# Delta rule of a hybrid encoder block: the inverse kept on the other half of the partitions than its transpose, PSUM banks exchanged

## The chip, the core and the metric

The kernel runs on one core of a Trainium2 chip. The core has a matrix engine (TensorE, PE in the rows, its weight loads PEld), VectorE (DVE), ScalarE (ACT), GpSimd (POOL) and SyncE (SP), which here issues most transfers. TensorE reads both operands from SBUF, where a tile lies on up to 128 partitions, and writes PSUM, which has eight banks. The operand's partitions choose the rows of the array that a product uses, the output's partitions choose its columns. So a product of 64 rows and 64 columns uses one quarter of the array. The metric is device time in microseconds of one execution; lower is better.

## The reference

One encoder block over 1024 tokens of 1024 channels: layer norm and modulation, one input projection, two mixers (gated delta rule, window attention), gates, output projection, layer norm, a hierarchical mixture of experts, layer norm. What the change touches is the delta rule. In chunks of 64 tokens and for 8 heads it needs the solution of a unit lower triangular system:

```python
decay = jnp.where(causal, jnp.exp(jnp.where(causal, gdiff, 0.0)), 0.0)
lower = jnp.where(strict, jnp.einsum('bnhid,bnhjd->bnhij', k_beta, kc) * decay, 0.0)
tmat = lower + jnp.eye(CHUNK, dtype=f32)
u = lax.linalg.triangular_solve(tmat, v_beta, left_side=True, lower=True, unit_diagonal=True)
w = lax.linalg.triangular_solve(tmat, k_beta * jnp.exp(gc)[..., None],
                                left_side=True, lower=True, unit_diagonal=True)
attn = jnp.einsum('bnhid,bnhjd->bnhij', qc, kc) * decay
...
v_new = u_n - jnp.einsum('bhcd,bhde->bhce', w_n, state)
```

followed by a state of 128x128 per head that goes from chunk to chunk.

## The kernel before

`delta_rule` takes the tokens in eight steps `c` of 128 tokens. Each step holds two chunks of 64 tokens, one on partitions 0 to 63 and one on 64 to 127 (`rows[0]` and `rows[1]`, line 1124), for eight heads side by side. All of it is float32.

The inverse T of the triangular matrix is built by doubling. `t_` holds T, `tt` holds its transpose. Both start from the 2x2 blocks on the diagonal: `lower` on VectorE makes `ln` (the negated lower matrix, line 1423), masks it (line 1425) and adds the identity to give `t_` (line 1427). `turn` on TensorE (line 1211) transposes it, and ScalarE copies it to `tt` (line 1343). Then five levels follow. A level `k` is:

1. TensorE: `cm` (the part of `ln` that belongs to the level, line 1418) times `tt`, into bank `g` (line 1223), for head groups `g` = 0 and 1 of four heads each.
2. ScalarE: copy of that to `nsb` (line 1348), one copy for each `g`.
3. TensorE, for each `g`: the update of `tt` (line 1234, `t_` by `nsb`) into the left half of bank 2+g, and for levels 1 to 4 the update of `t_` (line 1238, `nsb` by `t_`) into the right half of the same bank.
4. VectorE, for each `g`: add the two to `tt` (line 1442) and `t_` (line 1444).

Every product here has 64x64 weights and 64 moving columns. A product of chunk 0 reads partitions 0 to 63 and writes 0 to 63, one of chunk 1 reads and writes 64 to 127, so all products of the levels use the two quarters on the diagonal of the array. A float32 product is issued as two weight loads and two matmuls, so 8 products (4 heads, 2 chunks) are 16 matmuls in the trace.

Between the levels the order on TensorE, written out by hand at lines 1288 to 1312, puts the recurrence of the step before: `read_state` (line 1269) before level 1 and after level 2, `write_state` (line 1281 for the state, line 1284 for the output) after levels 1 and 3, `turn_output` (line 1259) and `value_rows` (line 1246) after level 4, and `key_rows` (line 1253) after level 5. Then come `similarities` (line 1186), `solutions` (lines 1194 and 1201) and `turn` of the next step. Line 1284 takes its operands from one half of the partitions and writes the other half (`rows[1 - s]`): it uses one of the two quarters off the diagonal. ScalarE copies the output rows after levels 2 and 4 (`output_rows`, line 1362), which `turn_output` needs. In step 0 VectorE also finishes a convolution (line 1473), whose result goes to DRAM and comes back as the value tiles that `value_rows` reads. GpSimd scales the queries (line 1536) and the state (line 1528). Engines are in step through semaphores alone.

Of the kernel before, what the change touches and what calls it, by code (L numbers as in the profile page):

```python
# [11 lines left out]
ALU = mybir.AluOpType  # L12
# [14 lines left out]
LEVELS = 6  # L27
# [1067 lines left out]
def delta_rule(nc, m, a):  # L1095

    with ExitStack() as ctx:
# [6 lines left out]
        cm, at = m.sb("level_parts", [P, 2, H, CHUNK], ctx=ctx), m.sb("attention_t", [P, 2, H, CHUNK], ctx=ctx)  # L1104
        t_, tt, nsb, ttb, ttw = chunked("inverse"), chunked("inverse_t"), chunked("level_product"), chunked("inverse_t_beta"), chunked("inverse_t_gc")
# [9 lines left out]
        S = lambda name: sems[name]  # L1115
# [6 lines left out]
        v_in = [m.sem(f"delta_v_in{side}") for side in range(2)]  # L1122
        ps = m.ps
        rows = [slice(0, CHUNK), slice(CHUNK, P)]
        ps4 = lambda b: ps[:, b, :].rearrange("p (h t) -> p h t", h=4)
        ps8 = lambda b: ps[:, b, :].rearrange("p (h t) -> p h t", h=H)
        part4 = lambda b, half: ps[:, b, half * 256:half * 256 + 256].rearrange("p (h t) -> p h t", h=4)
        heads = lambda g: slice(4 * g, 4 * g + 4)
        at8 = lambda h: slice(h * CHUNK, (h + 1) * CHUNK)
        at4 = lambda h, half=0: slice(half * 256 + (h % 4) * CHUNK, half * 256 + (h % 4 + 1) * CHUNK)  # L1130
# [5 lines left out]
        over = lambda name, k=0: m.const(name)[:, k * CHUNK:(k + 1) * CHUNK].rearrange("p (o t) -> p o t", o=1).to_broadcast([P, H, CHUNK])  # L1136
# [39 lines left out]
        def _(pe):  # L1176
# [27 lines left out]
            def turn(c):  # L1204
                pe.wait_ge(S("t0_ok"), c + 1)
                if c >= 1:
                    pe.wait_ge(S("n_ok"), c * 10)
                for g in range(2):
                    for h in range(4 * g, 4 * g + 4):
                        for r in rows:  # L1210
                            last = pe.matmul(ps[r, g, at4(h)], t_[r, h, :], m.const("ident_chunk")[r, :], start=True, stop=True)
                    last.then_inc(S("tt_mm"), 1)

            def level(c, k):
                pe.wait_ge(S("cm_ok"), c * 5 + k)
                for g in range(2):
                    if k == 1:
                        pe.wait_ge(S("tt0_ok"), c * 2 + g + 1)
                    else:
                        pe.wait_ge(S("tt_ok"), c * 10 + 2 * (k - 2) + g + 1)  # L1220
                    for h in range(4 * g, 4 * g + 4):
                        for r in rows:
                            last = pe.matmul(ps[r, g, at4(h)], cm[r, k % 2, h, :], tt[r, h, :], start=True, stop=True)  # L1223
                    last.then_inc(S("n_mm"), 1)
                if k == 1:
                    pe.wait_ge(S("ln_ok"), c + 1)
                    pe.wait_ge(S("at_ok"), c + 1)
                for g in range(2):
                    pe.wait_ge(S("n_ok"), c * 10 + 2 * (k - 1) + g + 1)
                    if k > 1:  # L1230
                        pe.wait_ge(S("t_ok"), c * 8 + 2 * (k - 2) + g + 1)
                    for h in range(4 * g, 4 * g + 4):
                        for r in rows:
                            last = pe.matmul(ps[r, 2 + g, at4(h)], t_[r, h, :], nsb[r, h, :], start=True, stop=True)
                    if k < LEVELS - 1:
                        for h in range(4 * g, 4 * g + 4):
                            for r in rows:
                                last = pe.matmul(ps[r, 2 + g, at4(h, 1)], nsb[r, h, :], t_[r, h, :], start=True, stop=True)
                    last.then_inc(S("x_mm"), 1)

            def value_rows(c):
# [46 lines left out]
            for c in range(TC):  # L1288
                similarities(c)
                if c >= 1:  # L1290
                    solutions(c - 1)
                turn(c)
                if c >= 1:
                    read_state(c - 1, 0)
                level(c, 1)
                if c >= 1:
                    write_state(c - 1, 0)
                level(c, 2)
                if c >= 1:
                    read_state(c - 1, 1)  # L1300
                level(c, 3)
                if c >= 1:
                    write_state(c - 1, 1)
                level(c, 4)
                if c >= 1:
                    turn_output(c - 1)
                if c >= 1:
                    value_rows(c)
                level(c, 5)
                if c == 0:  # L1310
                    value_rows(c)
                key_rows(c)
# [88 lines left out]
        def _(dve):  # L1401
# [13 lines left out]
            def part(c, k):  # L1415
                if k >= 3:
                    dve.wait_ge(S("n_mm"), c * 10 + 2 * (k - 2))
                nc.vector.tensor_tensor(cm[:, k % 2], ln[:], over("level", k), ALU.mult).then_inc(S("cm_ok"), 1)

            def lower(c):  # L1420
                dve.wait_ge(S("scaled_ok"), c + 1)
                dve.wait_ge(S("kk_mm"), c + 1)
                nc.vector.tensor_tensor(ln[:], ps8(2), ds_[:], ALU.mult).then_inc(S("ln_ok"), 1)
                dve.wait_ge(S("ln_ok"), c + 1)
                step(nc.vector.tensor_tensor(cm[:, 0], ln[:], over("level", 0), ALU.mult))
                step.settle()
                nc.vector.tensor_tensor(t_[:], cm[:, 0], over("ident_chunk"), ALU.add).then_inc(S("t0_ok"), 1)
                part(c, 1)
                dve.wait_ge(S("qk_mm"), c + 1)
                dve.wait_ge(S("dt_ok"), c + 1)  # L1430
                if c >= 2:
                    dve.wait_ge(S("o_mm"), 2 * (c - 1))
                nc.vector.tensor_tensor(at[:, c % 2], ps8(3), dt_[:], ALU.mult).then_inc(S("at_ok"), 1)

            def level(c, k):
                if k < LEVELS - 1:
                    if k == 1:
                        dve.wait_ge(S("t0_ok"), c + 1)
                    part(c, k + 1)
                for g in range(2):  # L1440
                    dve.wait_ge(S("x_mm"), c * 10 + 2 * (k - 1) + g + 1)
                    nc.vector.tensor_tensor(tt[:, heads(g), :], part4(2 + g, 0), tt[:, heads(g), :], ALU.add).then_inc(S("tt_ok"), 1)
                    if k < LEVELS - 1:
                        nc.vector.tensor_tensor(t_[:, heads(g), :], part4(2 + g, 1), t_[:, heads(g), :], ALU.add).then_inc(S("t_ok"), 1)

            def decayed_keys(c):
                dve.wait_ge(S("tok_mm"), c * 2 + 2)
# [34 lines left out]
            scale_decays(0)  # L1482
            for c in range(TC):
                lower(c)
                if c == 0:
                    for t in range(3):
                        convolve_last(0, t)
                if c >= 1:
                    new_values(c - 1, 0)
                level(c, 1)  # L1490
                if c == LAST - 1:
                    split_gates_low(nc, m, dve, 0, slice(0, 1))
                if c >= 1:
                    new_state(c - 1, 0)
                if c == 0:
                    convolve_last(1, 0)
                level(c, 2)
                if c == 0:
                    convolve_last(1, 1)
                if c == LAST - 1:  # L1500
                    split_gates_low(nc, m, dve, 0, slice(1, 2))
                if c >= 1:
                    new_values(c - 1, 1)
                level(c, 3)
                if c == 0:
                    convolve_last(1, 2)
# [1026 lines left out]
def build(nc, a, out):  # L2533
    with ExitStack() as ctx:
# [20 lines left out]
        with ExitStack() as mid:  # L2555
# [6 lines left out]
            with ExitStack() as early:  # L2562
# [25 lines left out]
                m.gate_in = [nc.alloc_semaphore(name=f"w_gates_in{n}") for n in range(2)]  # L2588
                m.gate_hi, m.gate_lo, m.gate_mm = (nc.alloc_semaphore(name="gates_" + n) for n in ("high_ready", "low_ready", "summed"))
                delta_rule(nc, m, a)  # L2590
                attended.close()
                m.reuse_sems()
# [36 lines left out]
```

## Time and profile before

| what | value |
|---|---|
| runs | 2004.98 us median of 3 (2002.21 to 2007.64) |
| span of the profiled execution | 2006.3 us |
| TensorE busy | 1834.1 us, 91% |
| VectorE busy | 1433.6 us, 71% |
| ScalarE busy | 1071.1 us, 53% |
| GpSimd busy | 358.4 us, 18% |
| delta rule in the span | from 578.6 us to about 902 us |

For the profiled execution only the span is given, from its first to its last instruction; it lies 1.3 us above the median of the runs and inside their range, so differences of the span are taken as differences of the time. The granted clock of TensorE was 0.96 of full speed on average. The busy time of a matmul row runs to its modelled end, so of a dense run of matmuls the distance from start to start is to be read, not the mean duration. The rows read for the prediction stand below.

### The profile page before, as it was taken

The page shows a single profiled execution, that of the slowest core. Times are in us where ns is not written, and L with a number is a line of the kernel's source. Part 1 is how long each engine was busy: PE and PEld are TensorE (multiplying, and loading weights), DVE is VectorE, ACT ScalarE, POOL GpSimd, SP SyncE. Part 2 cuts the span into 40 slices and gives each one's busy share as a digit, 9 for nine tenths or more (in the row PEclk, how much of TensorE's full clock was granted, in tenths as well). Part 3 has the DMA queues.
Part 4 walks back from the last instruction along what each step waited for, and adds up shares of the span by engine and source line. Part 5 has one row for each costly group of instructions (what it writes and reads, how often), then busy time and mean ns, then how long its engine had stood idle before and what let it go on. Part 6 is the DMA issues. An engine that isn't in the chain of part 4 may idle for free. (4 is left out here: it accounts for less than half of the span.)

```text
span 2006.3 us, 35312 instructions
## 1 busy us (share of the span) xinstructions
PE 1834.1 (91%) x14136; PEld 1043.3 (52%) x14136; DVE 1433.6 (71%) x1790; ACT 1071.1 (53%) x1310; POOL 358.4 (18%) x230
## 2 busy tenths in 40 slices
PE   4988869999978999989999999579999999999965
PEld 1655554444447999974444445434444444444432
DVE  5455555777776666736575768779999988888938
ACT  3455553355343333324333411278888888888934
POOL 0000000111101112110000000014444444444400
PEclk9999979999999999999999999689999999999988
DMA  8500007573444312106132321389999999999935
GB/s 319 101 22 22 1 1 283 189 252 126 173 114 121 88 50 71 29 2 202 53 105 57 111 74 74 137 328 396 404 404 414 409 397 402 390 394 387 363 133 204
DMA packets 161716, 391.32 MB, mean 195 GB/s; under 512 B 25371, under 2 KB 102804, under 8 KB 132910
## 3 DMA queue, kind: packets, MB, share of 16 engines
q1 hardware_dynamic: 146574, 357.87, 49.4%
q0 software_dynamic: 15008, 31.56, 4.2%
q8 instruction: 96, 1.57, 0.3%
q14 instruction: 38, 0.31, 0.1%
HBM read 361.68 MB, written 48.68 MB: 205 GB/s over the span
## 5 line engine op out<-in xcount | busy, mean ns | idle before, releaser
L2281 PE MATMUL ps<-w_gate_up_split,gathered_t 128*128 128x512 f16 x1728 | 388.5, 382 | 8.9 <-ACT gathered_t L2355 5.1
L2447 DVE SCALAR_TENSOR_TENSOR w_gate_up_split<-w_staged,w_gate_up_split 128x2048 f16<-128x2048 f32 x144 | 328.0, 2288 | 58.3 <-ACT w_gate_up_split L2346 56.8
L2346 ACT ACTIVATE w_gate_up_split<-w_staged 128x2048 f16<-128x2048 f32 x144 | 274.6, 1908 | 48.7 <-PE ps L2281 14.5
L2281 PEld LDWEIGHTS ps<-w_gate_up_split,gathered_t 128*128 128x128 f16 x1728 | 167.8, 98 | 209.1 <-ACT gathered_t L2355 10.5
L219 PE MATMUL ps<-u_transposed,w_gates_split 128*128 128x512 f16 x1152 | 254.7, 383 | 5.8 <-PEq L144 3.0
L825 PE MATMUL ps<-u_transposed,w_dense_split 128*128 128x512 f16 x1152 | 250.5, 379 | 1.7 <-DVE w_dense_split L190 0.9
L2308 PE MATMUL ps<-w_down_split,hidden_t 128*128 128x512 f16 x864 | 195.8, 384 | 7.8 <-ACT hidden_t L2392 4.4
L219 PEld LDWEIGHTS ps<-u_transposed,w_gates_split 128*128 128x128 f16 x1152 | 113.3, 99 | 146.9 <-issue 14.8
L825 PEld LDWEIGHTS ps<-u_transposed,w_dense_split 128*128 128x128 f16 x1152 | 111.9, 98 | 142.3 <-issue 7.1
L2447 DVE SCALAR_TENSOR_TENSOR w_down_split<-w_staged,w_down_split 128x2048 f16<-128x2048 f32 x72 | 164.2, 2287 | 20.1 <-ACT w_down_split L2346 19.9
L2346 ACT ACTIVATE w_down_split<-w_staged 128x2048 f16<-128x2048 f32 x72 | 137.2, 1908 | 45.4 <-DMA w_staged<-in_w_down 23.0
L2308 PEld LDWEIGHTS ps<-w_down_split,hidden_t 128*128 128x128 f16 x864 | 83.6, 99 | 105.3 <-issue 8.3
L190 DVE SCALAR_TENSOR_TENSOR w_dense_split<-w_dense_ring,w_dense_split 128x512 f16<-128x512 f32 (+2 forms) x29 | 41.0, 1413 | 110.5 <-ACT w_dense_split L182 110.5
L1348 ACT ACTIVATE level_product<-ps 128x256 f32<-128x256 f32 x80 | 30.7, 384 | 145.6 <-PE ps L1223 143.5
L2237 POOL DMA_INDIRECT slots_scratch<-block_output,slot_row_now x36 | 47.4, 1316 | 330.2 <-ACT block_output L2364 321.8
L1737 ACT ACTIVATE gate_sigmoids<-ps 128x1024 f32<-128x1024 f32 x24 | 24.5, 1024 | 144.5 <-PE ps L219 144.5
L498 PE MATMUL ps<-u_transposed,w_dense_split 128*128 128x512 f16 x384 | 90.0, 380 | 0.0
L952 DVE SCALAR_TENSOR_TENSOR delta_output<-w_gates_split,vector_columns,delta_output 128x1024 f32<-128x1024 f32 x66 | 83.8, 1283 | 7.0 <-ACT delta_output L888 5.4
L2223 POOL DMA_INDIRECT gathered<-u_scratch,slot_token_now x34 | 79.4, 2334 | 29.0 <-POOL slot_token_now L2220 29.0
L1671 PE MATMUL ps<-w_out_split,delta_output 128*128 128x512 f16 x384 | 84.0, 379 | 0.0
L1085 POOL DMA_DIRECT2D qkv_scratch<-delta_output x20 | 11.1, 555 | 393.1 <-ACT delta_output L895 393.1
L1968 POOL MEMSET gathered<- 128x4096 f16 x1 | 3.5, 3512 | 410.1 <-POOLq L1551 410.1
(359 smaller groups left out, 3003.6 us busy)
## 6 DMA issues: line engine op xcount, KB each, us to landing
w_staged<-in_w_gate SPq DMA_DIRECT2D x72, 1024.0 KB, 11.8
w_staged<-in_w_up SPq DMA_DIRECT2D x72, 1024.0 KB
w_staged<-in_w_down SPq DMA_DIRECT2D x72, 1024.0 KB, 11.7
w_dense_ring<-in_w_in SPq DMA_DIRECT2D x17, 1024.0 KB, 7.6
w_ada_ring<-in_w_ada SPq DMA_DIRECT2D x8, 2048.0 KB
w_gates_ring<-in_w_in SPq DMA_DIRECT2D x24, 512.0 KB, 6.4
qkv_scratch<-delta_output POOLq DMA_DIRECT2D x20, 512.0 KB, 3.8
attention_output<-qkv_scratch SPq DMA_DIRECT2D x8, 1024.0 KB, 6.1
```

The costliest lines, as they stand in the source:

```text
L190: nc.vector.scalar_tensor_tensor(m.w16[:, i % 2, 1, ks, 0:n], m.w_ring[:, i % 2, ks, 0:n], W_SCALE, m.w16[:, i % 2, 0, ks, 0:n], ALU.mult, ...
L219: last = pe.matmul(m.ps[:, 2 * j + half, :], m.gate16[n % 2][:, j, wp, k, :], m.u[:, up, k, half * 512:half * 512 + 512], start=(t == 0), ...
L498: last = pe.matmul(ps[:, bank, :], w16[:, i % 2, wp, k, (j % 2) * P:(j % 2 + 1) * P], m.u[:, up, k, half * 512:half * 512 + 512], start=(t ...
L825: last = pe.matmul(ps[:, 2 * b + half, :], w16[:, (FIRST + p) % 2, i, k, b * P:(b + 1) * P], m.u[:, j, k, half * 512:half * 512 + 512], st ...
L952: last = nc.vector.scalar_tensor_tensor(acc[:, b, :], raw[:, b, 1 + t:1 + t + T], conv[:, t, n:n + 1], acc[:, b, :], ALU.mult, ALU.add)
L1671: last = pe.matmul(ps[:, y_bank(c) + half, :], merged(k, op)[:, c * P:(c + 1) * P], m.w_out[:, wp, k, half * 512:half * 512 + 512], start= ...
L2223: pool.indirect_dma_start(xg[:, s].rearrange("p h d -> p (h d)"), None, m.u2_dram.rearrange("t h d -> t (h d)"), bass.IndirectOffsetOnAxis ...
L2237: pool.indirect_dma_start(m.y_dram, bass.IndirectOffsetOnAxis(ap=row[:, s:s + 1], axis=0), y[:, s, :], None, bounds_check=2 * T - 1, oob_i ...
L2281: last = pe.matmul(ps[:, GU[s] + j, :], xt[:, s, xp, k, :], w16[:, j, wp, k, :], start=(k == 0 and t == 0), stop=(k == KC - 1 and t == 2))
L2308: last = pe.matmul(ps[:, 6 + half, :], ht[:, s, hp, k, :], wd16[:, wp, k, half * 512:half * 512 + 512], start=(k == 0 and t == 0), stop=(k ...
L2346: nc.scalar.activation(split(kind, 0, int(q)), staged(m, kind, int(q)), ACT.Identity, scale=W_SCALE).then_inc(hi_ok[kind + q], 1)
L2447: nc.vector.scalar_tensor_tensor(split(kind, 1, int(q)), staged(m, kind, int(q)), W_SCALE, split(kind, 0, int(q)), ALU.mult, ALU.subtract) ...
```

## The change

`t_` now lies crossed: chunk 0 of it on partitions 64 to 127 and chunk 1 on 0 to 63; `tt`, `ln` and `cm` stay where they were. The first product of a level writes crossed, so `nsb` lies crossed too. The update of `tt` reads the crossed half and writes the straight one (the quarters off the diagonal), the update of `t_` reads and writes the crossed half (the quarters on it). The two are now interleaved head by head. The update of `tt` goes to bank `g`, which the first product used before, the update of `t_` to bank 2+g. `turn` waits for `tt_ok` instead of `n_ok`, and the identity is added in two VectorE instructions of 64 partitions each, because each moves its half across.

```diff
+        crossed = [(rows[0], rows[1]), (rows[1], rows[0])]
...
             def turn(c):
                 pe.wait_ge(S("t0_ok"), c + 1)
                 if c >= 1:
-                    pe.wait_ge(S("n_ok"), c * 10)
+                    pe.wait_ge(S("tt_ok"), c * 10)
                 for g in range(2):
                     for h in range(4 * g, 4 * g + 4):
-                        for r in rows:
-                            last = pe.matmul(ps[r, g, at4(h)], t_[r, h, :], m.const("ident_chunk")[r, :], start=True, stop=True)
+                        for r, q in crossed:
+                            last = pe.matmul(ps[r, g, at4(h)], t_[q, h, :], m.const("ident_chunk")[q, :], start=True, stop=True)
...
             def level(c, k):
                     for h in range(4 * g, 4 * g + 4):
-                        for r in rows:
-                            last = pe.matmul(ps[r, g, at4(h)], cm[r, k % 2, h, :], tt[r, h, :], start=True, stop=True)
+                        for r, q in crossed:
+                            last = pe.matmul(ps[q, g, at4(h)], cm[r, k % 2, h, :], tt[r, h, :], start=True, stop=True)
...
                     for h in range(4 * g, 4 * g + 4):
-                        for r in rows:
-                            last = pe.matmul(ps[r, 2 + g, at4(h)], t_[r, h, :], nsb[r, h, :], start=True, stop=True)
-                    if k < LEVELS - 1:
-                        for h in range(4 * g, 4 * g + 4):
-                            for r in rows:
-                                last = pe.matmul(ps[r, 2 + g, at4(h, 1)], nsb[r, h, :], t_[r, h, :], start=True, stop=True)
+                        for r, q in crossed:
+                            last = pe.matmul(ps[r, g, at4(h)], t_[q, h, :], nsb[q, h, :], start=True, stop=True)
+                        if k < LEVELS - 1:
+                            for r, q in crossed:
+                                last = pe.matmul(ps[q, 2 + g, at4(h)], nsb[q, h, :], t_[q, h, :], start=True, stop=True)
                     last.then_inc(S("x_mm"), 1)
...
-                nc.vector.tensor_tensor(t_[:], cm[:, 0], over("ident_chunk"), ALU.add).then_inc(S("t0_ok"), 1)
+                for r, q in crossed:
+                    last = nc.vector.tensor_tensor(t_[q], cm[r, 0], over("ident_chunk")[r], ALU.add)
+                last.then_inc(S("t0_ok"), 1)
...
-                    nc.vector.tensor_tensor(tt[:, heads(g), :], part4(2 + g, 0), tt[:, heads(g), :], ALU.add).then_inc(S("tt_ok"), 1)
+                    nc.vector.tensor_tensor(tt[:, heads(g), :], part4(g, 0), tt[:, heads(g), :], ALU.add).then_inc(S("tt_ok"), 1)
                     if k < LEVELS - 1:
-                        nc.vector.tensor_tensor(t_[:, heads(g), :], part4(2 + g, 1), t_[:, heads(g), :], ALU.add).then_inc(S("t_ok"), 1)
+                        nc.vector.tensor_tensor(t_[:, heads(g), :], part4(2 + g, 0), t_[:, heads(g), :], ALU.add).then_inc(S("t_ok"), 1)
```

## Rows read from the trace of the kernel before

**Rows 1.** The page's head and the row of its first part for TensorE.
```profile
span 2006.3 us, 35312 instructions
...
PE 1834.1 (91%) x14136; PEld 1043.3 (52%) x14136; DVE 1433.6 (71%) x1790; ACT 1071.1 (53%) x1310; POOL 358.4 (18%) x230
```

**Rows 2.** Windows, one per step: length; busy PE, PEld, DVE, ACT, POOL; clock; DMA.
```profile
578.61:618.24 39.63, 23.93 (x560) 22.63 (x560) 28.72 (x43) 13.92 (x23) 4.93 (x3) 0.85 0.50 115
618.24:655.32 37.08, 36.34 (x729) 34.04 (x729) 23.59 (x43) 12.57 (x26) 7.51 (x4) 0.97 0.44 110
...
691.53:727.75 36.22, 35.47 (x730) 33.18 (x729) 23.98 (x44) 12.57 (x26) 7.51 (x4) 1.00 0.26 68
```

**Rows 3.** Timeline of TensorE, step 3, level 2: start us, length us, what.
```profile
705.88 1.63 PE L1284 MATMUL ps<-v_new,attention_t 64*64 64x128 f32 x13
707.24 0.27 PE L1223 MATMUL ps<-inverse_t,level_parts 64*64 64x64 f32 x2
707.35 0.27 PE L1284 MATMUL ps<-v_new,attention_t 64*64 64x128 f32 x1
707.35 0.28 PE L1223 MATMUL ps<-inverse_t,level_parts 64*64 64x64 f32 x4
707.45 0.27 PE L1284 MATMUL ps<-v_new,attention_t 64*64 64x128 f32 x1
707.47 0.28 PE L1223 MATMUL ps<-inverse_t,level_parts 64*64 64x64 f32 x4
...
707.58 0.81 PE L1223 MATMUL ps<-inverse_t,level_parts 64*64 64x64 f32 x22
708.47 0.68 PE L1234 MATMUL ps<-level_product,inverse 64*64 64x64 f32 x16
708.98 0.63 PE L1238 MATMUL ps<-inverse,level_product 64*64 64x64 f32 x16
...
709.91 0.63 PE L1238 MATMUL ps<-inverse,level_product 64*64 64x64 f32 x16
710.48 0.38 PE L1269 MATMUL ps<-state,w_and_q 128*128 128x128 f32 x1
```

**Rows 4.** Timeline of all engines, step 3, level 3 and what follows it.
```profile
712.46 1.15 PE L1223 MATMUL ps<-inverse_t,level_parts 64*64 64x64 f32 x32
...
713.19 0.85 ACT L1348 ACTIVATE level_product<-ps 128x256 f32<-128x256 f32 x2 [3.32 <-PE ps L1223]
...
713.62 0.68 PE L1234 MATMUL ps<-level_product,inverse 64*64 64x64 f32 x16
...
716.42 0.68 DVE L1406 TENSOR_TENSOR decay_steps<-token_scalars,decay_rows 128x512 f32<-128x512 f32 x1
...
717.86 2.93 POOL L1536 TENSOR_TENSOR w_and_q<-attention_output 128x512 f32<-128x512 f32 x2 [8.23 <-PE ps L1281]
```

**Rows 5.** Timeline of all engines, step 3, level 4 and the turning of the output.
```profile
720.20 0.68 PE L1234 MATMUL ps<-level_product,inverse 64*64 64x64 f32 x16
...
720.46 1.00 ACT L1362 ACTIVATE output_rows<-ps 64x1024 f32<-64x1024 f32 x1
...
722.22 1.09 PE L1259 MATMUL ps<-table,output_rows 128*128 128x128 f32 x8
```

**Rows 6.** Timeline of TensorE after the last level of step 7: line 1284 alone.
```profile
886.53 1.96 PE L1284 MATMUL ps<-v_new,attention_t 64*64 64x128 f32 x16
888.42 1.90 PE L219 MATMUL ps<-u_transposed,w_gates_split 128*128 128x512 f16 x8
```

**Rows 7.** Timeline of all engines ahead of the turn of step 4.
```profile
731.51 0.69 DVE L1427 TENSOR_TENSOR inverse<-level_parts,table 128x512 f32<-128x512 f32 x1
...
733.59 1.15 PE L1211 MATMUL ps<-table,inverse 64*64 64x64 f32 x32
```

**Rows 8.** Timeline of TensorE, end of step 0.
```profile
614.64 1.97 PE L1246 MATMUL ps<-table,attention_output 128*128 128x128 f32 x8 [4.33 <-DMA attention_output<-qkv_scratch]
```

**Rows 9.** Timeline of VectorE, step 6, after level 3.
```profile
826.91 1.64 DVE L1408 TENSOR_TENSOR decay_s<-decay_steps,table 128x512 f32<-128x512 f32 x1
```

## The prediction

> **What bounds the kernel now.** I read the page first, to see that TensorE is the busiest engine with 91% of the span [rows 1], and then the windows, one per step of the delta rule, because a share over the whole span says nothing of this stage. In a steady step TensorE has matmuls under way in 35.47 of 36.22 us, at the full granted clock of 1.00, that is 2.4 GHz, while VectorE has 23.98 and ScalarE 12.57 [rows 2]. So steps 1 to 7 go by the length of TensorE's queue, and what shortens it shortens the step. Step 0 is different: TensorE is busy in 23.93 of 39.63 us and VectorE leads with 28.72 [rows 2]; its end is a wait of 4.33 us for the value tiles to come back from DRAM [rows 8].
>
> The next question is what the queue costs, read from start to start. In level 2 of step 3 the updates run from 708.47 to 710.48, where the next kind of product begins: 64 matmuls in 2.01 us. From the first start of line 1238 at 708.98 to its second at 709.91 there are 32 matmuls in 0.93 us, 29.1 ns each; two quarters share the work, so one quarter takes a matmul each 58.2 ns [rows 3]. 64 matmuls at 29.1 ns are 1.86 us, and 0.15 us are left for the changeover to another shape.
>
> Is that 58.2 ns the quarter's own time, or the time in which TensorE takes up instructions? The place where three quarters have work answers it. Line 1284 (off the diagonal) starts a matmul of 128 columns at 707.35 and the next at 707.45. In between and beside it line 1223 (on the diagonal) starts 4 matmuls of 64 columns at 707.35 and 4 more at 707.47, which is 0.12 us for two in each quarter, no slower than without company [rows 3]. So quarters that share rows, and quarters that share columns, run side by side at full pace, and one matmul starts each 23 ns or so. Products queued later also start before earlier ones in another quarter: line 1223 begins at 707.24, before line 1284 has started its last three.
>
> **The change part by part.** *The two updates on four quarters.* Per level 1 to 4 and step, 64 matmuls that now take 29.1 ns take 14.6 ns if all four quarters work: 0.93 us instead of 1.86, and with the changeover 1.08 us instead of 2.01. That is 0.93 us per level and 3.72 us per step. No row shows four quarters at work. The bounds are 14.6 ns (each quarter keeps its 58.2) and 29.1 ns (the fourth and third add nothing); I take 14.6, since the nearest row has three at full pace. Level 5 has one update alone and keeps its time.
>
> Is each update's input there in time? ScalarE's two copies start at 713.19 and last 0.85 us, to 714.04; the update started at 713.62, so the second head group's copy is there 0.42 us after the start. The first group's 32 matmuls now take 0.47 us, so the second is not held up, by 0.05 us [rows 4]. If it were, by up to 0.1 us in each of 28 levels, 2.8 us would be lost. VectorE's additions begin earlier too, since the first group is signalled after 0.47 instead of 0.93 us; between levels TensorE has 2 to 3.7 us of other work for them to hide under.
>
> *Level 4 and the output rows.* After level 4 `turn_output` needs ScalarE's copy of line 1362. It began 0.26 us after the update and lasted 1.00 us; TensorE got there 2.02 us after the update began (720.20 to 722.22), so it never waited [rows 5]. Now TensorE arrives after 1.08 us. In a level without overlap the copies end at 0.42 us [rows 4], so line 1362 ends at 1.42 or so: 0.35 us of the gain turn into a wait, at least 0.2 (with 1.26 for its end) and at most 0.45 us.
>
> *The overlap that goes.* Line 1223 moves from the diagonal to the quarters off it, one of which line 1284 is using at that time. The head start seen in rows 3 needs free quarters, and in program order the busy one holds it back. Before, from the start of line 1284 to the start of the update took 2.59 us (705.88 to 708.47) [rows 3]. Line 1284 alone takes 1.89 us with its changeover (886.53 to 888.42) [rows 6], 1.74 without, and line 1223 to the update 1.16 us (712.46 to 713.62) [rows 4]: 3.05 or 2.90 us. The loss is 0.31 to 0.46 us; I take 0.38, as one changeover may or may not be paid. It comes twice per step, after levels 1 and 3: 0.77 us.
>
> *The identity in two instructions.* The one instruction takes 0.69 us [rows 7]; a half of the partitions costs between half of that and the same, and I take the same, as the number of elements per partition stays: 0.7 us later. TensorE started the turn at 733.59, the instruction ended at 732.20 [rows 7]; 1.39 us of slack in `solutions` hide it in steps 1 to 7. Without that cover it would be 0.7 us per step, 5 us in all. In step 0 VectorE leads and the last convolution, its store and reload follow, so TensorE's 4.33 us wait [rows 8] moves by 0.7 us, and what the levels gain in that step is lost in the same wait.
>
> *VectorE and GpSimd.* The decays began 2.80 us after the update (716.42) and GpSimd's line 1536 4.24 us after it (717.86) [rows 4]. Both come earlier, GpSimd's by the whole 0.93 us and VectorE's by less, so that they meet. In step 6 they met before, and line 1408 took 1.64 us [rows 9] against 0.68 of its like [rows 4]. One or two instructions 1 us longer fit into VectorE's slack in an ordinary step; in step 6, which has other work too, I set 0.3 us (0 to 1).
>
> *Waits and banks.* `turn` waits for additions that `similarities` has waited for already: nothing. The exchange of banks adds no wait, since the update of a group needs the copy out of its bank anyway. No DMA and no queue of SyncE is touched.
>
> *Sum.* Per steady step 3.72 - 0.35 - 0.77 = 2.60 us. Seven steps: 18.2 us. Less 0.7 in step 0 and 0.3 in step 6: 17.2 us. The profiled span of 2006.3 us [rows 1] becomes 1989.1; from the median of 2004.98 it is 1987.8, and I say 1988. What follows the delta rule is issued after it and moves along.
>
> **The rivals.** *Four quarters give nothing (slower).* If rows or columns of the array can serve only what two quarters need once the fourth one joins, the updates keep 1.86 us and the losses stay: 7 x 0.77 + 0.7 = 6.1 us, 2011. It decides by the pace in the updates: with 4 x 64 matmuls per step the losses of 0.87 us per step are covered below 25.7 ns per matmul. Against it stands that both kinds of sharing run at full pace with three [rows 3]; for it, that the fourth was never seen. Chance 0.13.
>
> *Three at a time.* To start all four, TensorE must look past the second matmuls of three waiting products. The rows show it past three waiting ones of line 1284 [rows 3], which is less sure for more. With three, a matmul starts each 19.4 ns: 0.62 us less per level, 2.48 - 0.77 = 1.71 per step, 11.3 in all, 1994. Chance 0.08.
>
> *Supply.* The fast stretch is some 10 matmuls long [rows 3] and may have been fed from what had piled up behind line 1284. If TensorE takes up instructions in the long run no faster than one matmul each 23 ns, a level gains 64 x 6 ns = 0.39 us, a step 1.56 - 0.77 = 0.79, all 4.8 us: 2000. If half of each update is fed from the pile, a level gains 0.47 us, a step 1.1, and the time is 1998. Chance 0.10 for both.
> The Trainium skill ("TensorE: Matmul & The Clock Gate", the section on the 56 ns gap) states a floor of about 25 ns from start to start, however few the columns. By it a step would gain 4 x 64 x 4.1 = 1.05 us before its losses, and the time would be 2003 to 2004; the stretch with a start each 23 ns is just below that floor, so the trace does not bear it out as a rule over quarters.
>
> *Clock.* In step 0 TensorE idles more between shorter bursts; a granted clock of 0.85 there and 0.97 in step 1 [rows 2] shows that halved stretches occur. One more of them in a step that TensorE bounds would cost 2 to 4 us. Chance of enough of them to matter 0.03.
>
> **How the numbers follow.** The forecast has 0.66: 1988, by its bounds 1985 (nothing waits in level 4) to 1992 (second copy late, more lost with GpSimd). Three at a time 0.08 at 1994, supply 0.10 at 1998 to 2004, nothing 0.13 at 2010 to 2012, clock 0.03. The range of 1984 to 1999 holds the forecast, the three quarters and half of supply, and leaves out about 0.2. A measurement of this kernel can tell 0.3%, or 6 us, from no change. Faster by more than that, below 1999: 0.66 + 0.08 + 0.05, 0.79. Slower, above 2011: half of the 0.13 and some of the clock, 0.08. Between: 0.13.
>
> **What the profile after would show.** In the updates one start per 14.6 ns, and 1.08 us from the start of the update to the next shape in levels 1 to 3. A wait of 0.35 us of line 1259 for line 1362. Lines 1284 and 1223 one after the other, 2.9 to 3.05 us to the update. Steady steps of 33.6 us in the windows instead of 36.2. The turn of the steps 1 to 7 not waiting for the identity, and step 0 about 0.7 us longer. The prediction is wrong if the update's pace is not near 14.6 ns, if the second copy holds it up, or if steps lengthen at places that wait for VectorE now.

## The result: 1985.3 us, ratio 0.9906

The changed kernel takes 1985.34 us (median of 4 runs, 1981.48 to 1987.67) against 2003.83 us (2002.21 to 2007.64) for the kernel before in the same comparison: a ratio of 0.9906, 95% interval 0.9888 to 0.9923. That is 18.5 us less, where 17.2 were forecast. The profiled span went from 2006.3 [rows 1] to 1985.7 us.

The head of the page and TensorE's row, and the windows of step 0, step 1 and step 3 (length; busy PE, PEld, DVE, ACT, POOL; clock; DMA), to be held against [rows 1, 2]:

```profile
span 1985.7 us, 35320 instructions
...
PE 1810.5 (91%) x14136; PEld 1020.4 (51%) x14136; DVE 1436.4 (72%) x1798; ACT 1071.3 (54%) x1310; POOL 358.4 (18%) x230
```

```profile
578.44:618.04 39.60, 22.80 (x560) 21.48 (x560) 29.40 (x44) 13.79 (x23) 4.92 (x3) 0.72 0.53 113
618.04:652.25 34.21, 33.38 (x730) 31.01 (x729) 23.85 (x44) 12.57 (x26) 7.54 (x4) 0.97 0.50 121
...
685.68:719.12 33.44, 32.61 (x729) 30.24 (x729) 24.25 (x45) 12.57 (x26) 7.55 (x4) 1.00 0.28 74
```

A steady step is 33.44 us instead of 36.22, 2.78 us less with the same number of matmuls, and TensorE is still busy in 32.61 of it: the stage is as much bound by TensorE's queue as before, the queue is only shorter.

Where the 2.78 us come from shows in TensorE's timeline, level 3 of step 3 (start us, length us, what):

```profile
706.25 0.27 PE L1235 MATMUL ps<-level_product,inverse 64*64 64x64 f32 x2
706.27 0.27 PE L1238 MATMUL ps<-inverse,level_product 64*64 64x64 f32 x2
706.36 0.23 PE L1235 MATMUL ps<-level_product,inverse 64*64 64x64 f32 x2
706.38 0.22 PE L1238 MATMUL ps<-inverse,level_product 64*64 64x64 f32 x2
706.42 0.22 PE L1235 MATMUL ps<-level_product,inverse 64*64 64x64 f32 x2
706.43 0.23 PE L1238 MATMUL ps<-inverse,level_product 64*64 64x64 f32 x2
...
707.35 2.05 PE L1281 MATMUL ps<-v_new,k_decayed 64*128 64x128 f32 x16
```

Two matmuls of each update start together, one in each of the four quarters. The second four follow after 0.11 us, which was so before as well, and from then on four start every 58 ns up to the end of the update: 14.6 ns each, against 29.1 before [rows 3]. The first start is at 706.25, the next shape begins at 707.35, so the 64 matmuls with the changeover take 1.10 us (1.09 in level 2) instead of 2.01.

Level 4 shows what the change costs (level 2 is much alike up to the update). TensorE's timeline, ScalarE's, and TensorE's wait behind level 4, all of step 3:

```profile
709.33 1.63 PE L1284 MATMUL ps<-v_new,attention_t 64*64 64x128 f32 x13
710.69 0.27 PE L1224 MATMUL ps<-inverse_t,level_parts 64*64 64x64 f32 x1
...
711.01 0.27 PE L1284 MATMUL ps<-v_new,attention_t 64*64 64x128 f32 x1
711.02 1.20 PE L1224 MATMUL ps<-inverse_t,level_parts 64*64 64x64 f32 x29
712.22 0.27 PE L1235 MATMUL ps<-level_product,inverse 64*64 64x64 f32 x2
```

```profile
712.53 1.00 ACT L1362 ACTIVATE output_rows<-ps 64x1024 f32<-64x1024 f32 x1
...
713.59 1.09 PE L1259 MATMUL ps<-table,output_rows 128*128 128x128 f32 x8 [0.21 <-ACT output_rows L1362]
```

Only three matmuls of the first product (one in level 2) start before line 1284 has started its last, where before the product had ten under way [rows 3]; from the start of line 1284 to the update it is 712.22 - 709.33 = 2.89 us, in level 2 it is 2.92 us, against 2.59 before [rows 3]. And after level 4 the turn of the output comes 1.37 us after the update, not 1.10: it waits for ScalarE.

The sum of a steady step by the traces: 0.92, 0.92 and 0.91 us in the updates of levels 1 to 3 and 0.65 in level 4, less 0.33 and 0.30 for the overlap: 2.77 us, which is the whole difference but for rounding.

### The profile page after: what moved, and what is told of

The parts are those of the page before. It is cut to its first block and busy times, and to the rows that moved or that the text cites. A ratio compares the mean times of both kernels' runs of the same rounds, so it can differ in the third digit from the quotient of the medians.

```text
span 1985.7 us, 35320 instructions
## 1 busy us (share of the span) xinstructions
PE 1810.5 (91%) x14136; PEld 1020.4 (51%) x14136; DVE 1436.4 (72%) x1798; ACT 1071.3 (54%) x1310; POOL 358.4 (18%) x230
## 5 line engine op out<-in xcount | busy, mean ns | idle before, releaser
L2449 DVE SCALAR_TENSOR_TENSOR w_down_split<-w_staged,w_down_split 128x2048 f16<-128x2048 f32 x72 | 164.2, 2287 | 17.4 <-ACT w_down_split L2348 17.2
```

What stands on the lines that cost most here:

```text
L2449: nc.vector.scalar_tensor_tensor(split(kind, 1, int(q)), staged(m, kind, int(q)), W_SCALE, split(kind, 0, int(q)), ALU.mult, ALU.subtract) ...
```

## The experiments

Each was compared with the kernel before, run beside it, in three sessions, whose medians for the kernel before lie between 2002.7 and 2003.8 us; "step" is the distance from the first start of `similarities` in step 3 to that in step 4.

| kernel | median us | ratio (95% interval) | steady step | step 6 |
|---|---|---|---|---|
| before | 2002.7 to 2003.8 | 1 | 36.21 | 36.21 |
| changed | 1985.3 | 0.9906 (0.9888 to 0.9923) | 33.44 | 34.24 |
| in_turn | 1995.3 | 0.9962 (0.9946 to 0.9977) | 34.76 | 34.91 |
| by_two | 1986.1 | 0.9918 (0.9898 to 0.9938) | 33.58 | 34.32 |
| before_straight | 2007.9 | 1.0029 (1.0019 to 1.0040) | 36.84 | 36.84 |
| straight | 1981.2 | 0.9886 (0.9866 to 0.9906) | 32.89 | 33.78 |
| identity_late | 1989.7 | 0.9941 (0.9924 to 0.9957) | 34.04 | 34.84 |
| values_first | 1982.4 | 0.9902 (0.9885 to 0.9918) | 33.16 | 35.07 |
| woven | 1969.8 | 0.9833 (0.9812 to 0.9853) | 31.05 | 34.42 |
| woven_later | 1964.6 | 0.9810 (0.9793 to 0.9826) | 30.81 | 30.81 |

**Is it the four quarters, and must the products be neighbours?** In `in_turn` everything of the change stays but the mixing:

```diff
                         for r, q in crossed:
                             last = pe.matmul(ps[r, g, at4(h)], t_[q, h, :], nsb[q, h, :], start=True, stop=True)
-                        if k < LEVELS - 1:
+                    if k < LEVELS - 1:
+                        for h in range(4 * g, 4 * g + 4):
                             for r, q in crossed:
```

> The changed kernel, with the two updates of a head group again one after the other (all products of the tt update, then all of the t_ update) instead of head by head; halves, banks and waits stay. Theory (the gain comes from four quarters being at work at once, and TensorE looks only a few products ahead in its queue): the two updates overlap only where one ends and the next begins, some 0.1 us at each of three joints of a level, so a level keeps 1.7 of the 2.01 us of before, a steady step is about 35.6 us against 33.4 in the changed kernel, and the time about 2000 us. Rival 1 (the quarters are fed independently, however far apart their products are queued): the step stays 33.4 us and the time 1985. Rival 2 (the gain is in the banks, the signals and VectorE's earlier additions, not in the quarters): between 1985 and 1990.

Measured: a step of 34.76 us and 1995.3 us. Not 35.6 and 2000 as my theory had it, and far from 33.4, so both rivals fall: with halves, banks and waits as in the change, about half of the gain goes when the two updates are queued one after the other. TensorE's timeline of `in_turn`, level 1 of step 3, shows the look-ahead itself (line 1235 is the update of `tt`, line 1239 that of `t_`):

```profile
697.18 0.51 PE L1235 MATMUL ps<-level_product,inverse 64*64 64x64 f32 x10
697.47 0.27 PE L1239 MATMUL ps<-inverse,level_product 64*64 64x64 f32 x2
...
698.23 0.51 PE L1239 MATMUL ps<-inverse,level_product 64*64 64x64 f32 x11
698.67 2.05 PE L1282 MATMUL ps<-v_new,k_decayed 64*128 64x128 f32 x16
```

The second update begins when 10 of the 16 matmuls of the first have started: TensorE starts work for free quarters past six waiting matmuls, three in each of the two busy quarters. The update takes 698.67 - 697.18 = 1.49 us, so each of three joints saves 0.17 us where I had set 0.1. The size of the look-ahead was off, not its being short. Four updates of 0.52 us less each, minus the 0.63 us of lost overlap, make 1.44 us, and the step of `in_turn` is 1.45 us below the kernel before: nothing is left over for banks, signals or earlier additions.

`by_two` mixes the updates by pairs of heads, four products of one and then four of the other:

```diff
-                    for h in range(4 * g, 4 * g + 4):
-                        for r, q in crossed:
-                            last = pe.matmul(ps[r, g, at4(h)], t_[q, h, :], nsb[q, h, :], start=True, stop=True)
-                        if k < LEVELS - 1:
-                            for r, q in crossed:
+                    for pair in ((4 * g, 4 * g + 1), (4 * g + 2, 4 * g + 3)):
+                        for h in pair:
+                            for r, q in crossed:
+                                last = pe.matmul(ps[r, g, at4(h)], t_[q, h, :], nsb[q, h, :], start=True, stop=True)
+                        if k < LEVELS - 1:
+                            for h in pair:
+                                for r, q in crossed:
```

> The changed kernel with the two updates mixed by pairs of heads (tt for two heads, t_ for the same two, and so on), between head by head (1.10 us from an update to the next shape) and group by group (1.50 us, 0.17 us saved at each of three joints). Theory (TensorE's look-ahead is worth some 0.17 us of a quarter's work, three matmuls of 0.058 each, a block of two heads being four): most of a block is overlapped, 1.15 to 1.3 us for the update, a steady step of 33.6 to 34.2 us, 1987 to 1991 us. Rival (only immediate neighbours overlap): 1.5 us and 34.8 as with whole groups.

Measured: 33.58 us for a step, 0.14 more than head by head, and 1986.1 us (two runs), both just below what was expected. The update takes 1.14 us. A block of eight matmuls is almost within the look-ahead of six, and the rival that only immediate neighbours overlap falls. The 0.14 us per step are read from the trace; the two medians alone could not tell it.

**Does the first product lose its head start because of the quarter?** `before_straight` leaves the updates of the kernel before as they are and moves line 1284's product onto the diagonal, by letting u, w and the queries change halves:

```diff
-                    for r in rows:
-                        last = pe.matmul(ps[r, 4 + h // 4, wide4(h)], ttb[r, h, :], vt[r, h, :], start=True, stop=True)
+                    for s, r in enumerate(rows):
+                        last = pe.matmul(ps[rows[1 - s], 4 + h // 4, wide4(h)], ttb[r, h, :], vt[r, h, :], start=True, stop=True)
...
-                    last = pe.matmul(ps[rows[1 - s], 4 + 2 * s + h // 4, wide4(h)], at[r, c % 2, h, :], vn[r, h, :], start=False, stop=True,
+                    last = pe.matmul(ps[r, 4 + 2 * s + h // 4, wide4(h)], at[r, c % 2, h, :], vn[r, h, :], start=False, stop=True,
...
-                    last = nc.scalar.activation(wq[:, s, :, rows[s]], ps8(6 + s), ACT.Identity)
+                    last = nc.scalar.activation(wq[:, s, :, rows[1 - s]], ps8(6 + s), ACT.Identity)
...
-                    last = nc.vector.tensor_tensor(vn[r, heads(g), :], u[r, heads(g), :], ps[r, 4 + 2 * s + g, :].rearrange("p (h t) -> p h t", h=4), ALU.subtract)
+                    last = nc.vector.tensor_tensor(vn[r, heads(g), :], u[q, heads(g), :], ps[q, 4 + 2 * s + g, :].rearrange("p (h t) -> p h t", h=4), ALU.subtract)
...
-                    last = nc.gpsimd.tensor_tensor(wq[:, s, :, rows[1 - s]], tiles[:, c % 2, 0:H, r], eg[:, c % 2, :, r], ALU.mult)
+                    last = nc.gpsimd.tensor_tensor(wq[:, s, :, r], tiles[:, c % 2, 0:H, r], eg[:, c % 2, :, r], ALU.mult)
```

and the copies of the output rows likewise. `straight` is the same edit on the changed kernel, where the first product is off the diagonal.

> The kernel before, with one thing changed: the new values and the output rows of the recurrence change halves (solutions for u written crossed, w and q columns exchanged), so that line 1284's product runs on a quarter of the diagonal, where the first product of the level works too. The updates are as before. Theory (the head start of the first product before the end of line 1284 needs other quarters): it is lost in levels 2 and 4, 0.3 us each, a steady step goes from 36.2 to 36.8 us and the time from 2004 to 2008.5 us. Rival (the head start has to do with something else, the queue or the waits): step 36.2 us, time 2004.

> The changed kernel with the same exchange in the recurrence: line 1284 now on a quarter of the diagonal while the first product of a level is off it. Theory: the head start comes back, 0.3 us in levels 2 and 4; a steady step goes from 33.4 to 32.8 us, the time from 1985 to 1981 us. Rival (the head start needs more than other quarters): step 33.4 us, 1985.

Both came as forecast: a step of 36.84 (0.63 us more) and 2007.9 us, and a step of 32.89 (0.55 us less) and 1981.2 us. (The intervals of `straight` and of the changed kernel overlap; it is the steps of the traces that tell them apart.) Taking the head start away from the kernel before costs nearly the same as giving it back to the changed one gains, and the quarter of line 1284 is what decides. TensorE's timeline of `before_straight`, level 2 of step 3:

```profile
704.44 1.85 PE L1284 MATMUL ps<-v_new,attention_t 64*64 64x128 f32 x15
706.02 0.27 PE L1223 MATMUL ps<-inverse_t,level_parts 64*64 64x64 f32 x1
706.13 0.27 PE L1284 MATMUL ps<-v_new,attention_t 64*64 64x128 f32 x1
706.13 1.20 PE L1223 MATMUL ps<-inverse_t,level_parts 64*64 64x64 f32 x31
707.35 0.68 PE L1234 MATMUL ps<-level_product,inverse 64*64 64x64 f32 x16
```

From 704.44 to 707.35 it is 2.91 us, as in the changed kernel, against 2.59 [rows 3]. The gain of `straight` stays 0.08 us short of 0.63, since turn_output then waits longer for the output rows: 1.45 us after the start of the update of level 4 instead of 1.37.

**Is a quarter's own work the only limit?** `woven` is `straight` with the products of line 1284 queued between those of the first product (`write_state` now hands its eight output products to `level`, which queues one ahead of each pair of heads and the other four behind):

```diff
-            def level(c, k):
+            def level(c, k, out=()):
+                out = list(out)
...
                     for h in range(4 * g, 4 * g + 4):
+                        if h % 2 == 0 and out:
+                            out.pop(0)()
                         for r, q in crossed:
...
                     last.then_inc(S("n_mm"), 1)
+                while out:
+                    out.pop(0)()
...
-                if c >= 1:
-                    write_state(c - 1, 0)
-                level(c, 2)
+                level(c, 2, write_state(c - 1, 0) if c >= 1 else ())
```

> As straight, and the products of line 1284 are queued between those of the first product of levels 2 and 4 (one ahead of each pair of heads, the other four behind), so that three quarters work for the whole first product. Theory (a quarter's own work is the only limit, one matmul of 128 columns each 0.107 us beside two quarters with one of 64 each 0.058): from the start of line 1284 to the start of the update 1.75 to 1.8 us instead of 2.9 in the changed kernel, 1.1 us less in two levels of a step, a steady step 31.2 us, the time about 1970 us. Rival (VectorE becomes the bound: its decays, slowed by GpSimd, and the additions of levels 3 and 4 now have less cover): the step stays above 32 us with TensorE waiting in levels 4 and 5, and the time is 1976 or more.

Measured: a step of 31.05 us, 1969.8 us. TensorE's timeline, level 2 of step 3 (line 1290 is the output product, 1227 the first product of the level, 1240 and 1243 the updates):

```profile
691.78 0.27 PE L1290 MATMUL ps<-v_new,attention_t 64*64 64x128 f32 x1
691.79 0.28 PE L1227 MATMUL ps<-inverse_t,level_parts 64*64 64x64 f32 x4
691.89 0.27 PE L1290 MATMUL ps<-v_new,attention_t 64*64 64x128 f32 x1
691.91 0.28 PE L1227 MATMUL ps<-inverse_t,level_parts 64*64 64x64 f32 x4
...
692.98 0.27 PE L1240 MATMUL ps<-level_product,inverse 64*64 64x64 f32 x2
693.00 0.27 PE L1243 MATMUL ps<-inverse,level_product 64*64 64x64 f32 x1
693.09 0.27 PE L1290 MATMUL ps<-v_new,attention_t 64*64 64x128 f32 x1
```

Three quarters keep their pace together: one of the 128 columns each 0.11 us and four of 64 each 0.12. One detail differs from what I expected: the update begins already 1.37 us after line 1290, not 1.75, since it looks past the last output products, and takes 1.45 us, not 1.09, since one quarter still has three of them to do. The sum of 2.82 us is what that quarter has to do in either case.

Step 6 is 34.42 us, and there the rival holds. VectorE's timeline of `woven`, step 6:

```profile
794.20 1.76 DVE L1411 TENSOR_TENSOR decay_steps<-token_scalars,decay_rows 128x512 f32<-128x512 f32 x1
796.00 1.64 DVE L1413 TENSOR_TENSOR decay_s<-decay_steps,table 128x512 f32<-128x512 f32 x1
797.56 0.68 DVE L1414 SCALAR_TENSOR_TENSOR decay_t<-decay_steps,table 128x512 f32<-128x512 f32 x1
798.17 1.28 DVE L1475 TENSOR_TENSOR state<-ps,state_decayed 128x512 f32<-128x512 f32 x2
```

and TensorE's:

```profile
799.59 1.92 PE L1251 MATMUL ps<-table,attention_output 128*128 128x128 f32 x8 [1.61 <-DVE state L1475]
801.43 1.86 PE L1227 MATMUL ps<-inverse_t,level_parts 64*64 64x64 f32 x32
```

The value tiles wait 1.61 us for the state, which queues behind decays that take 1.76 and 1.64 us. That is half of the 3.4 us by which this step is longer than a steady one. The rest goes with the clock: the granted clock is 1.00 up to 799.6 and 0.72 from there to 805.8, that is, part of this stretch at 1.2 GHz, after some 4.6 us in which TensorE was busy for 2.8. From the value tiles to line 1227 it takes 1.84 us there instead of 0.97, the 32 matmuls of line 1227 take 1.86 us by their row instead of 1.15, and these places and the update behind them are 1.6 us longer together.

**What would the waits around it cost or give?** `identity_late` puts two VectorE instructions of 64 partitions ahead of the identity:

```diff
                 step(nc.vector.tensor_tensor(cm[:, 0], ln[:], over("level", 0), ALU.mult))
+                for r, q in crossed:
+                    step(nc.vector.tensor_tensor(xs[q], ln[r], over("ident_chunk")[r], ALU.add))
                 step.settle()
```

> The changed kernel with two more VectorE instructions of 64 partitions (into a tile that is free then) ahead of the identity, 1.4 us. Theory: the turn of the steps 1 to 7 has 0.68 us of slack left (691.52 against 690.84 in the trace of the changed kernel), so it comes 0.72 us later and a steady step takes 34.15 us instead of 33.44; time 5 to 6 us more, 1991. Rival (the turn doesn't wait for the identity at all): 33.44 us and 1985; other rival (the change's own two instructions already hold it up): 34.8 us.

In the changed kernel the two instructions took 1.39 us and left slack: VectorE, then TensorE, ahead of the turn of step 3:

```profile
689.45 1.39 DVE L1428 TENSOR_TENSOR inverse<-level_parts,table 64x512 f32<-64x512 f32 x2
```

```profile
691.52 1.15 PE L1212 MATMUL ps<-table,inverse 64*64 64x64 f32 x32
```

In `identity_late` the row reads

```profile
691.26 1.15 PE L1212 MATMUL ps<-table,inverse 64*64 64x64 f32 x32 [0.73 <-DVE inverse L1430]
```

and the turn comes 6.64 us after the step's start instead of 5.84, 0.80 us later. The step grows by 0.60 us to 34.04, and the median by 4.3 us, a little under what was expected. VectorE ends 1.42 us later, so the cover was 0.62 us: the 0.68 as read less 0.05 us that lie between VectorE's end (691.21) and the turn. Of the 0.80 us, 0.2 are made up behind the turn: `read_state` starts 1.08 us after it instead of 1.30, where in the changed kernel it had started only 0.10 us after ScalarE's copies of w and the queries ended (7.04 us after the step's start in both kernels).

`values_first` swaps two calls:

```diff
+                if c >= 1:
+                    value_rows(c)
                 if c >= 1:
                     turn_output(c - 1)
-                if c >= 1:
-                    value_rows(c)
                 level(c, 5)
```

> The changed kernel with value_rows ahead of turn_output after level 4. Theory (after level 4 TensorE waits 0.27 us for ScalarE's copy of the output rows, 1.37 against 1.10 us, and it can turn the value tiles meanwhile): the wait goes, a steady step takes 33.17 us instead of 33.44, some 2 us in all, 1983; in step 6, where the values wait for the state, nothing or a small loss. Rival (key_rows, which waits for the turned output's copy, only waits longer): 33.44 us.

The steady step is 33.16 us, as expected. But step 6 is 35.07 instead of 34.24: TensorE waits 1.9 us there for the state, now that the output's turn no longer stands ahead. The net gain of the seven steps is below 1 us, and the medians (1982.4 against 1985.3, ratios 0.9902 and 0.9906 with intervals that overlap) don't tell the two kernels apart.

`woven_later` has this swap and moves the decays of the next step behind level 4 on VectorE and behind the output's copy on ScalarE:

```diff
                 level(c, 4)
+                if c < LAST:
+                    decays(c + 1)
                 level(c, 5)
```

> The woven kernel with value_rows first, and with the decays of the next step computed after level 4's additions on VectorE and after the output's copy on ScalarE, out of the stretch in which GpSimd slows them. Theory (in the woven kernel turn_output waits 0.6 us for ScalarE in each step, and step 6 takes 34.42 instead of 31.06 us because VectorE's decays, stretched by GpSimd, hold up the state that value_rows needs): a steady step of 30.4 us, step 6 of about 31 us, 7 us less than the woven kernel, 1962 to 1964. Rival (the decays, now nearer to their use, hold up the next step's lower matrix and the turn): a step longer than 31.06.

Measured: 30.81 us in the steady steps and in step 6 alike, 1964.6 us. Its windows of step 3 and step 6:

```profile
677.54:708.35 30.81, 30.22 (x729) 28.19 (x728) 24.46 (x45) 12.68 (x27) 7.09 (x4) 1.00 0.31 79
769.96:800.77 30.81, 30.21 (x729) 28.19 (x729) 27.64 (x48) 15.40 (x30) 7.16 (x4) 1.00 0.21 55
```

Step 6 gives back the whole 3.6 us, and the swap alone had made step 6 longer, so the place of the decays was its cause. The time is 0.6 us above the forecast. The steady step gained 0.24 us and not 0.6: I had taken the 1.71 us from the update of level 4 to `turn_output` in `woven` against 1.10, but 1.45 of it is the update itself in that kernel; only the rest was a wait. This kernel is the fastest of the ten: 0.9810 of the time before, 39 us less in the delta rule by the traces (259.6 us from the first product of the stage to the first gate product, against 298.9).

Left open: the mixed updates of a head group in one PSUM bank, as before, were not tried. So no run says whether the mixing needs the exchange of banks; that the exchange brings no time of its own follows from the sum for `in_turn`. The mixed order with `t_` on its old half was not tried either. There all four products fall on the two quarters of the diagonal, whose own work of 32 matmuls of 58.2 ns each is the 1.86 us of before; that this would stay is argued, not shown.

## Why the prediction was right, step by step

- *TensorE's queue bounds steps 1 to 7.* Right. The step lost 2.78 us of its length and 2.86 us of TensorE's busy time.
- *14.6 ns per matmul on four quarters.* Right, and the nearest row, three quarters at full pace [rows 3], was the right one to take the value from. The updates take 1.09 to 1.10 us where 1.08 were forecast. The second head group is not held up: in level 3 ScalarE's copies start at 705.82 and last 0.85 us, to 706.67, and the group starts at 706.77, 0.06 us after the matmuls before it. The rivals "nothing", "three at a time" and "supply" all fall with this row. The fast pace holds over all 64 matmuls, so the floor of about 25 ns from start to start in the Trainium skill ("TensorE: Matmul & The Clock Gate", the section on the 56 ns gap) does not hold over the four quarters together; the trace has 14.6 ns.
- *Look-ahead.* The forecast used it only in a rival. `in_turn` shows that half the gain hangs on the order in which the products are queued.
- *Overlap lost, 0.77 us per step (0.62 to 0.92).* 0.63 us, at the lower bound; `before_straight` measures the same 0.63 by itself. The mis-sized term is the changeover of line 1284: 0.15 us in [rows 6], where a product of another shape follows, and not paid where line 1224 follows, which is 64x64 too: 2.9 us, not 3.05.
- *Wait for the output rows, 0.35 us.* 0.27 us. ScalarE's copy began 0.31 us after the update and not 0.42, since it overlaps the copy before it.
- *Identity.* Two instructions take 1.39 us, 0.70 more, with 0.68 us of slack left, as worked out; `identity_late` found the edge of it.
- *VectorE and GpSimd meet.* The premise was wrong: the prediction has them meet in ordinary steps only after the change, but they had met there before. VectorE in step 3 of the kernel before:

```profile
719.55 1.78 DVE L1418 TENSOR_TENSOR level_parts<-minus_lower,table 128x512 f32<-128x512 f32 x1
```

  VectorE and GpSimd in step 3 of the changed kernel:

```profile
709.67 1.76 DVE L1409 SCALAR_TENSOR_TENSOR decay_t<-decay_steps,table 128x512 f32<-128x512 f32 x1
```

```profile
709.57 3.00 POOL L1538 TENSOR_TENSOR w_and_q<-attention_output 128x512 f32<-128x512 f32 x2 [6.72 <-PE ps L1281]
```

  Before, it was line 1418 that took 1.78 us, begun while GpSimd was at work from 717.86 on [rows 4]; now it is a decay with 1.76, and line 1418 is back at 0.68. Both kernels have one such instruction in each of steps 0 to 5 and two in step 6, so the change added none. In steady steps it stays hidden. In step 6 it costs 0.8 us, where I had set 0.3 within 0 to 1, and for another reason than mine: VectorE has the state ready 29.4 us after the step's start instead of 31.3, 1.8 us earlier, but TensorE would take it 2.8 us earlier (value tiles at 28.84 in step 3 instead of 31.61) and waits.
- *Step 0 longer by 0.7 us.* Not seen: 39.60 against 39.63 us. VectorE's part is there, as its last convolution ends 0.69 us later after the step's start, and the reload of the values was issued at 30.95 us instead of 30.03. But it landed faster: the first value product came 5.05 us after the issue instead of 5.99. Over the ten kernels with a trace this time lies between 4.17 and 6.01 us, whatever their change, and even the issue lies between 29.98 and 30.95 us in the seven kernels that have the two instructions and nothing more ahead of them. The spread of the transfer and of what runs before it is larger than the term, so these traces can't show it. TensorE's granted clock was lower in that step (0.72 of full speed against 0.85), and the step was no longer for it.
- *Clock.* In steps 2 to 6 the granted clock of the changed kernel is 1.00, so this rival did not come true here; it did in step 6 of `woven`, for 1.6 us.
- *The sum.* A steady step gives 2.77 us where 2.60 were forecast, since two losses were smaller (0.63 for 0.77 and 0.27 for 0.35), which is 1.2 us over seven steps. Step 0 cost nothing instead of 0.7 and step 6 cost 0.8 instead of 0.3; that these two misses nearly cancel is luck. So the whole was 18.8 us by the traces of the stage (298.9 to 280.1 us) against 17.2 forecast, and 18.5 by the medians. The rest of the 20.6 us between the two spans lies outside the delta rule, where the span differs by up to 5.4 us between these kernels, though none of them changes it.

## What to carry to other kernels

Small products should be laid so that neighbours in the queue fall on different quarters of the array: operands on one half of the partitions and outputs on the other give the two quarters off the diagonal; here that took one more instruction that moves a half across, and the overlap that another product had on those quarters. Count each quarter's own work, because in these traces the longest of the four is what a stretch takes; and ask of every product that changes its quarter what used to run beside it. What is gained on the bounding engine shows up next as waits on what used to be hidden, here the output rows and the decays. Moving those gave another 5.2 us (from `woven` to `woven_later`), more than giving line 1284 its head start back (4.2 us, from the changed kernel to `straight`).

## What the runs showed of the hardware that was not expected

TensorE starts matmuls for a free quarter past earlier ones that wait for a busy quarter, and in these traces past at most three for each busy quarter. That is six where two quarters are busy (`in_turn`: the second update starts when 10 of the 16 matmuls of the first have started) and three where line 1284 keeps one busy (13 of its 16 have started [rows 3]). The price of the order for the 64 matmuls of an update: 1.09 us head by head, 1.14 in blocks of eight, 1.49 in blocks of sixteen, 2.01 on two quarters.

VectorE's float32 instructions of 128x512 that read and write SBUF take 0.68 us; those that began while GpSimd was at work took 1.64 to 1.81 us. That holds for all of them in the delta rule of nine of the ten kernels, apart from some that began in the last 0.05 us of GpSimd's work; in `woven_later` five took 0.76 us and one 1.05. Those that had begun shortly before GpSimd's (line 1418 at 700.42, GpSimd at 700.58) kept their 0.68 us, and the additions that read PSUM kept their 0.41 us. No run was made to show why.
